# Zero matmuls in TensorE's waits, and ScalarE's tables held to the set with both Ln and Exp, in a two-block transformer kernel

## The chip, the core and the metric

The kernel runs on one core of one Trainium2 chip. TensorE multiplies into PSUM, VectorE and ScalarE read PSUM and work in SBUF, GpSimd helps VectorE, and DMA queues bring the weights from HBM. The metric is the device time of one execution in microseconds (us). Before the change it is 2707.82 us, the median of 3 runs (2706.88 to 2712.28).

## The reference

All is fp32, for 256 tokens of width 1024, in two blocks.

```python
# first block, layers l = 0, 1
x = x + (swa_sb_mixer(h, ...) if l == 0 else hgrn2_mixer(h, ...))   # h = rms_norm(x, norm_mix[l])
x = x + memory_cross_attention(rms_norm(x, norm_cross[l]), rms_norm(mem, norm_mem[l]), ...)
x = x + conv_ffn(rms_norm(x, norm_ffn[l]), ...)
# second block, i = 0, 1
h = pool_mixer(x, ...) if i == 0 else nsa_mixer(x, ...)
x = layer_norm(ALPHA * x + h, ln_g[i, 0], ln_b[i, 0])
f = swiglu(x, ...) if i == 0 else moe_ffn(x, ...)        # 8 experts, each token goes to 2
x = layer_norm(ALPHA * x + f, ln_g[i, 1], ln_b[i, 1])
```

The first mixer is a sliding-window softmax (8 heads) beside stick-breaking attention (8 heads: softplus, a reversed cumulative sum, exp). HGRN2 is gated linear attention with a decay. NSA has three branches: keys compressed by a small network, selected blocks, and a window; here the last two are causal attention over all 256 keys, 4 groups of 4 heads.

## The kernel before, in words

**Layout.** Activations stand with channels on the 128 partitions: `x` is 8 blocks of 256 tokens. All dense weights come as one stream of slots of 128x2048 fp32 (1 MB). SyncE loads a slot into one of 6 `raw` buffers, ScalarE rounds it to fp32r (`whi`, `split_hi`, line 458, 4 buffers), VectorE or GpSimd subtracts (`wlo`, lines 1294 and 426), and TensorE makes three matmuls of each product: high by high, high by low, low by high (`split_mm`, lines 722 to 724). The activations are split the same way into `hh` and `hl` (`to_hi`, `to_lo`, lines 1359 and 1362).

**Stages, in the order of the program.** ab_in (9 slots), sliding window, stick-breaking, ab_out (4); cross-attention with kv (8 slots), q (4), o (4); feed-forward (33); HGRN hg_in (16), its chunk products, hg_out (4); cross-attention and feed-forward again; then pool (1), LayerNorm 0, feed-forward, LayerNorm 1, nsa_in (10), the compressed branch, the NSA softmax, nsa_out (4), LayerNorm 2, router, 8 experts of 42 slots, LayerNorm 3. A projection slot is 48 matmuls of 128x256: 2 output blocks of 8 input blocks of 3.

**What sets the order.** Each engine runs its own list, written out by hand, and waits for semaphores. There is no scheduler. TensorE runs its list in order, so whatever stands in front of a wait is done before the wait is looked at, and whatever stands behind waits too.

**A norm.** VectorE squares (line 1338), TensorE sums over channels with a matrix of ones in fp32 (line 776; each such matmul is two instructions in the trace), ScalarE makes rstd as exp(-0.5 ln(sum)) (lines 471 and 472), VectorE scales (line 1372) and splits in four quarters (semaphore `h_ready`), and the first 24 matmuls of the next slot wait for these quarters one after the other. A LayerNorm (`layer_norm_pe`) has two such sums, of x and of the centred squares, and scales and shifts (lines 1401, 1406) before the split.

**Softmax stages** (`softmax_pe`, `softmax_act`, `softmax_dve`). In each step TensorE makes the scores of a unit of 4 heads (line 817), the transposes of the probabilities two units back (line 803) and the value product three units back (lines 846, 854, 857). VectorE masks and takes the maximum (lines 1432 to 1440), ScalarE makes four Exp (line 487) and then the copy of the transposes (line 496).

**ScalarE's tables.** The build puts an ACT_TABLE_LOAD ahead of an activation whose function is not in the set that is loaded. Where Ln and Exp follow each other it loads for each of them.

Of the kernel before, what the change touches and what calls it, by code (L numbers as in the profile page):

```python
# [14 lines left out]
P = 128  # L15
# [3 lines left out]
BLK = T  # L19
SLOT = 16 * P  # L20
QUARTERS = 4
# [81 lines left out]
def build(nc, stream, x_in, mem_in, pos_in, params, consts, stage_consts, w1_in, out):  # L103
    ctx = ExitStack()
    with ctx:
# [338 lines left out]
        def _(act):  # L444
# [22 lines left out]

            def norm_act(n, count, eps):
# [7 lines left out]

            def softmax_act(kind, u0):
                us = units(kind)
                for step in range(len(us) + 2):
# [11 lines left out]
                    if step >= 2:  # L491
# [4 lines left out]
                        nc.scalar.activation(r3(PT[u % 2], 4)[:, :, 0:nk], r3(banks(2), 4)[:, :, 0:nk], ACT.Copy).then_inc(pt_copied, 1)  # L496

            def ffn_act(layer, conv):
                for i in range(4):
# [5 lines left out]
                    for s in range(ph.n):  # L505
# [6 lines left out]
                        split_hi(ph.g + s + DEPTH)  # L512

# [32 lines left out]
            nc.scalar.activation(W(33, 2), W(33, 2), ACT.Sin).then_inc(sines_ready, 1)  # L546

# [36 lines left out]
            def log_decays():  # L584
                act.wait_ge(hg_sig, 1)
# [37 lines left out]
            nc.scalar.activation(W(24, 8), W(24, 8), ACT.Silu).then_inc(hg_gate, 1)  # L623
            for c in range(QUARTERS):
                act.wait_ge(hg_o, c + 1)
                nc.scalar.activation(hf[:, c * 512:(c + 1) * 512], ps[:, c, :], ACT.Square).then_inc(hg_osq, 1)
# [28 lines left out]
            ins.then_inc(cmp_silu, 1)  # L655
            act.wait_ge(cmp_shifted, 1)
# [45 lines left out]
            with act.Else():  # L702
# [9 lines left out]
                expert_pairs(act, expert)  # L712
            norm_act(11, D, 1e-5)
# [3 lines left out]
        def _(pe):  # L717
# [8 lines left out]
            def proj_slot(ph, s, e=0, h=None, odd=0):  # L726
# [15 lines left out]
            def proj_pe(name, h, then=None):  # L742

                ph = PHASES[name]
                for s in range(ph.n):
                    proj_slot(ph, s, h=h)
# [40 lines left out]
            def ffn_pe(layer, h):  # L787
                at_least(pe, acc_drained, QUARTERS * layer)
                for i in range(4):
                    ph = PHASES[f"ffn{layer}_{i}"]  # L790
                    if ph.kind == "gu":
                        for s in range(ph.n):
                            proj_slot(ph, s, h=h if i == 0 else None)
# [11 lines left out]
            def softmax_pe(kind, u0, o0, q_at, k_at, v_at, cmp=None):  # L805
                us = units(kind)
                branches = 2 if kind == "nsa" else 1
                for step in range(len(us) + 3):
                    if step < len(us):
                        u = u0 + step  # L810
                        g, qt, br = us[step]
                        nk = P * key_tiles(kind, qt)
                        at_least(pe, scores_masked, u)
# [16 lines left out]
                    if step >= 3:  # L830
# [3 lines left out]
                        kts = key_tiles(kind, qt)  # L834
# [1340 lines left out]
```

## Time and profile before

| | us |
|---|---|
| median of 3 runs | 2707.82 (2706.88 to 2712.28) |
| profiled execution | 2710.58 |
| its span, first to last instruction | 2708.8 |
| TensorE (PE) busy | 2463.7 (91%), 17928 instructions |
| VectorE (DVE) busy | 1854.6 (68%) |
| ScalarE (ACT) busy | 1322.4 (49%) |
| GpSimd (POOL) busy | 309.4 (11%) |
| mean granted clock of TensorE | 0.948 of full |

The granted clock has two levels: 1.00 is 2.4 GHz, 0.50 is 1.2 GHz. Busy TensorE counts pipelined matmuls that overlap, so it does not say that the array runs at its peak. PEld rows are weight loads. An idle time in brackets is that of the engine ahead of the row, and the name behind the arrow is what ended it. Idle time of an engine that nobody waits for costs nothing.

### The profile page before, as it was taken

The numbers are of one execution on the slowest core, as the hardware profiler recorded it, in microseconds if no ns is written. First come the engines' busy times: TensorE is split into PE (matmuls) and PEld (weight loads), VectorE is DVE, ScalarE is ACT, GpSimd is POOL, SyncE is SP. The second block draws the span as 40 slices with busy tenths as digits, with TensorE's granted clock in tenths as the row PEclk, the third lists the DMA queues.
The fourth block names the chain that finished last, engine by engine and source line by source line (L and its number), as shares of the span: only waits on it lengthen the run. The fifth ranks groups of instructions, "written<-read, shape, count | busy, mean of one in ns | idle before, by whom it ended". The sixth has DMA issues, their size and how long they took to land.

```text
span 2708.8 us, 43109 instructions
## 1 busy us (share of the span) xinstructions
PE 2463.7 (91%) x17928; PEld 2323.5 (86%) x17928; DVE 1854.6 (68%) x2338; ACT 1322.4 (49%) x1432; POOL 309.4 (11%) x70
## 2 busy tenths in 40 slices
PE   6779789988887899699988888999999999999997
PEld 6579789988887899699987568999999999999996
DVE  5655466668565675723355657888888888888887
ACT  4443333344433333233321435766767677676764
POOL 0000054500000364163400000000000000000000
PEclk9789899999998899899988799999999999999998
DMA  5124135442341355355531015988989998899995
GB/s 210 63 80 154 63 141 187 179 143 107 108 150 63 125 184 179 110 182 181 187 109 47 1 63 200 362 339 327 353 333 343 344 343 344 340 345 342 342 341 207
DMA packets 77087, 556.69 MB, mean 206 GB/s; under 512 B 8544, under 2 KB 8672, under 8 KB 9952
## 3 DMA queue, kind: packets, MB, share of 16 engines
q1 hardware_dynamic: 75888, 547.45, 54.8%
q10 hardware_dynamic: 1008, 6.49, 0.6%
q8 instruction: 145, 2.38, 0.3%
q14 instruction: 46, 0.38, 0.1%
HBM read 552.86 MB, written 1.05 MB: 204 GB/s over the span
## 4 chain that ended last, share of the span: by engine, by line
PE 61%; DVE 4%; ACT 2%; issue 1%; DMA 0%; ACTq 0%; DVEq 0%
PE ps L1169 11%; PE ps L1171 11%; PE ps L1170 11%; PE ps L722 6%; PE ps L723 6%; PE ps L724 6%; PE ps L803 2%; PE ps L776 1%; PE ps L1209 1%; PE ps L1163 1%; PE ps L857 1%; PE ps L817 1%; PE ps L854 1%; ACT whi L458 0%; PE ps L1081 0%
## 5 line engine op out<-in xcount | busy, mean ns | idle before, releaser
L458 ACT ACTIVATE whi<-raw 128x2048 fp32r<-128x2048 f32 x519 | 994.1, 1916 | 658.0 <-PE ps L724 505.4
L1294 DVE TENSOR_TENSOR wlo<-raw,whi 128x2048 fp32r<-128x2048 f32 x453 | 1035.0, 2290 | 226.1 <-ACT whi L458 225.4
L722 PE MATMUL ps<-hh,whi 128*128 128x256 f32 x2336 | 678.8, 291 | 98.6 <-DVE hl L1362 90.2
L723 PE MATMUL ps<-hl,whi 128*128 128x256 f32 x2336 | 672.1, 288 | 0.0
L724 PE MATMUL ps<-hh,wlo 128*128 128x256 f32 x2336 | 671.5, 287 | 0.0
L722 PEld LDWEIGHTS ps<-hh,whi 128*128 128x128 f32 x2336 | 460.0, 197 | 105.0 <-issue 103.2
L1169 PE MATMUL ps<-whi,hh 128*128 128x256 f32 x1792 | 523.4, 292 | 3.6 <-DVE work L1939 3.6
L1171 PE MATMUL ps<-wlo,hh 128*128 128x256 f32 x1792 | 507.7, 283 | 0.0
L1170 PE MATMUL ps<-whi,hl 128*128 128x256 f32 x1792 | 507.6, 283 | 0.0
L723 PEld LDWEIGHTS ps<-hl,whi 128*128 128x128 f32 x2336 | 460.4, 197 | 0.3
L724 PEld LDWEIGHTS ps<-hh,wlo 128*128 128x128 f32 x2336 | 459.8, 197 | 0.0
L426 POOL TENSOR_TENSOR wlo<-raw,whi 128x2048 fp32r<-128x2048 f32 x66 | 309.2, 4684 | 1018.3 <-ACT whi L458 1018.3
L1169 PEld LDWEIGHTS ps<-whi,hh 128*128 128x128 f32 x1792 | 343.4, 192 | 4.4 <-DVE work L1939 3.8
L1170 PEld LDWEIGHTS ps<-whi,hl 128*128 128x128 f32 x1792 | 344.7, 192 | 0.6
L1171 PEld LDWEIGHTS ps<-wlo,hh 128*128 128x128 f32 x1792 | 344.1, 192 | 0.0
L1169 PE MATMUL ps<-whi,ahi 128*128 128x512 f32 x448 | 180.8, 404 | 0.0
L1171 PE MATMUL ps<-wlo,ahi 128*128 128x512 f32 x448 | 174.7, 390 | 0.0
L1170 PE MATMUL ps<-whi,alo 128*128 128x512 f32 x448 | 174.6, 390 | 0.0
L723 PE MATMUL ps<-alo,whi 128*128 128x256 f32 x528 | 149.4, 283 | 0.0
L724 PE MATMUL ps<-ahi,wlo 128*128 128x256 f32 x528 | 149.4, 283 | 0.0
L722 PE MATMUL ps<-ahi,whi 128*128 128x256 f32 x528 | 149.4, 283 | 0.0
L686 ACT ACTIVATE work<-ps 128x128 f32<-128x128 f32 x224 | 62.3, 278 | 165.3 <-PE ps L1171 165.2
(319 smaller groups left out, 2681.1 us busy)
## 6 DMA issues: line engine op xcount, KB each, us to landing
raw<-stream SPq DMA_DIRECT2D x519, 1024.0 KB, 4.8
work<-w_in ACTq DMA_DIRECT2D x1, 2240.0 KB, 8.4
stage<-stage_consts ACTq DMA_DIRECT2D x4, 512.0 KB, 4.8
work<-mem_in ACTq DMA_DIRECT2D x2, 1024.0 KB, 4.8
x<-x_in SPq DMA_DIRECT2D x1, 1024.0 KB, 4.9
out<-x SPq DMA_DIRECT2D x4, 256.0 KB, 2.3
const<-consts SPq DMA_DIRECT2D x1, 548.5 KB, 5.8
par<-params SPq DMA_DIRECT2D x1, 405.5 KB, 6.4
```

Of the source, the lines that this page charges most:

```text
L426: nc.gpsimd.tensor_tensor(wlo[g % RAWS][:, :], raw[g % RAWS][:, :], whi[hi_at(g, odd)][:, :].bitcast(F32), ALU.subtract).then_inc(lo_ready ...
L458: nc.scalar.activation(whi[hi_at(g, odd)][:, :], raw[g % RAWS][:, :], ACT.Copy).then_inc(hi_ready, 1)
L686: nc.scalar.activation(Wc(FEW_GATE + P * bank, P), ps[:, bank, 0:P], ACT.Silu).then_inc(gate_act, 1)
L722: mm(out_ap, hi_w, hi_x, start=start, stop=False, **kw)
L723: mm(out_ap, hi_w, lo_x, start=False, stop=False, **kw)
L724: return mm(out_ap, lo_w, hi_x, start=False, stop=stop, **kw)
L776: last = mm(ps[:, bank, 0:BLK], C("ones"), src[:, b * BLK:(b + 1) * BLK], start=(b == 0), stop=(b == NB - 1))
L803: return nc.tensor.transpose(dst, src, C("ident"))
L1169: mm(out_ap, hi_x, hi_w, start=start, stop=False, **kw)
L1170: mm(out_ap, lo_x, hi_w, start=False, stop=False, **kw)
L1171: return mm(out_ap, hi_x, lo_w, start=False, stop=stop, **kw)
L1294: V.tensor_tensor(wlo[g % RAWS][:, :], raw[g % RAWS][:, :], whi[hi_at(g, odd)][:, :].bitcast(F32), ALU.subtract).then_inc(lo_ready[g % RAW ...
```

## The change

**TensorE.** `keep_warm(bank, n)` issues n matmuls of a tile of zeros (128x128) by zeros (256 columns, fp32r) into a bank that nobody reads at that time. It stands ahead of waits: 12 to 32 at the start of projections (with `norm`, 6 ahead of a wait for rstd, the rest behind it), 4 ahead of each group of scores, transposes and values in the sliding window and in NSA, 8 in cross-attention, 12 and 8 in stick-breaking, 24 and 16 in pool, 14 to 24 between the sums of a LayerNorm, and a few more. They are 948 in all. A few waits are new or come earlier (`xa_rstd`, `hg_orstd`, `rstd_ready`, `dup_copied`), each of something that a later wait implies.

**ScalarE.** `load_log_exp` loads the set that has both Ln and Exp, `load_exp` the set of Exp that the softmaxes had before. After them the build finds the functions loaded and adds nothing. 43 loads run where 61 ran. The first layer is not restored after the sliding window, so norms 1 and 2, stick-breaking and the first cross-attention load as before. VectorE's, GpSimd's and SyncE's lists are the same.

```diff
+            def load_log_exp():
+
+                act.preload_act_table_set("natural_log_exp_and_others")
...
+            def load_exp():
+
+                act.preload_act_table_set("exp_and_others")
+
             def softmax_act(kind, u0):
+                load_exp()
...
+                if kind != "swa":
+                    load_log_exp()
...
                         split_hi(ph.g + s + DEPTH)
+                    if i == 2:
+                        load_log_exp()
...
             def log_decays():
+                load_log_exp()
...
             nc.scalar.activation(W(24, 8), W(24, 8), ACT.Silu).then_inc(hg_gate, 1)
+            load_log_exp()
...
+            def keep_warm(bank, n):
+
+                for _ in range(n):
+                    mm(ps[:, bank, 0:BLK], zero[:, :], zero[:, :].unsqueeze(1).to_broadcast([P, 2, P]), start=True, stop=True)
+
-            def proj_slot(ph, s, e=0, h=None, odd=0):
+            def proj_slot(ph, s, e=0, h=None, odd=0, idle=0, norm=None):
...
+                if norm is not None:
+                    keep_warm(bank, 6)
+                    pe.wait_ge(rstd_ready, norm + 1)
+                keep_warm(bank, idle)
...
-            def layer_norm_pe(i, wait):
+            def layer_norm_pe(i, wait, idle):
                 sums_pe(x, MEAN_BANK[i], wait).then_inc(mean_ready, 1)
+                keep_warm(7, idle)
                 norm_pe(8 + i)
...
+                def warm(step, n):
+                    if kind != "xa":
+                        keep_warm(7, n)
+                    elif step < 3:
+                        keep_warm(4, 2 * n)
...
+                        if step:
+                            warm(step, 4)
                         at_least(pe, scores_masked, u)
...
+                        warm(step, 4)
                         pe.wait_ge(probs_ready, u + 1)
...
+                        warm(step, 4)
                         pe.wait_ge(pt_copied, u + 1)
...
+                pe.wait_ge(xa_rstd, 3 * layer + 3)
+                keep_warm(4, 20)
                 pe.wait_ge(heads_ready, 2 + layer)
...
-            proj_pe("hg_in", 7, {s: lambda s=s: after_hg_slot(s) for s in range(7, hg.n)})
+            proj_pe("hg_in", 7, idle=22, norm=4, then={s: lambda s=s: after_hg_slot(s) for s in range(7, hg.n)})
             pe.wait_ge(banks_drained, hg.e + hg.n)
+            keep_warm(0, 10)
...
-            proj_pe("hg_out", 8, {1: lambda: norm_pe(5)})
+            pe.wait_ge(hg_orstd, QUARTERS)
+            keep_warm(7, 16)
+            proj_pe("hg_out", 8, then={1: lambda: norm_pe(5)})
...
-            ffn_pe(1, 12)
+            ffn_pe(1, 12, norm=7, idle=22)
+            keep_warm(7, 24)
...
             for g in range(4):
+                keep_warm(7, 16 if g else 24)
                 pe.wait_ge(h_ready, QUARTERS * 12 + g + 1)
...
+            keep_warm(7, 10)
             pe.wait_ge(cmp_kv_copied, 1)
             mm(ps[:, 3, 0:60], C("rot"), small[:, 288:348], start=True, stop=True).then_inc(cmp_rot, 1)
+            keep_warm(7, 8)
             pe.wait_ge(cmp_roped, 1)
...
-            layer_norm_pe(3, lambda c: pe.wait_ge(acc_drained, QUARTERS * 3 + c + 1))
+            keep_warm(7, 8)
+            layer_norm_pe(3, lambda c: pe.wait_ge(acc_drained, QUARTERS * 3 + c + 1), 20)
```

TensorE's list from the end of the first feed-forward over norm 4 to hg_in, before (line 767 closes the accumulation, 776 is the norm's sums, 722 to 724 the projection):

```order
L767 MATMUL ps<-zero 128x512 x4
L776 MATMUL ps<-hf,const 128x256 x8
L722 MATMUL ps<-hh,whi_63 128x256
L723 MATMUL ps<-hl,whi_63 128x256
L724 MATMUL ps<-hh,wlo_57 128x256
```

and with the change, where the same lines are 794, 803 and 740 to 742, and 747 is `keep_warm`:

```order
L794 MATMUL ps<-zero 128x512 x4
L747 MATMUL ps<-zero 128x256 x10
L803 MATMUL ps<-hf,const 128x256 x8
L747 MATMUL ps<-zero 128x256 x28
L740 MATMUL ps<-hh,whi_63 128x256
L741 MATMUL ps<-hl,whi_63 128x256
L742 MATMUL ps<-hh,wlo_57 128x256
```

Ten stand ahead of the sums, 6 + 22 between them and the first matmul that waits for h.

ScalarE's list at the HGRN output norm, before (626 squares, 630 is Ln, 633 Exp):

```order
L623 ACTIVATE work<-work 128x2048
L626 ACTIVATE hf<-ps 128x512 x4
L630 ACT_TABLE_LOAD
L630 ACTIVATE work<-ps,const 128x512 x4
L633 ACT_TABLE_LOAD
L633 ACTIVATE work<-work 128x512 x4
```

and with the change:

```order
L638 ACTIVATE work<-work 128x2048
L470 ACT_TABLE_LOAD
L642 ACTIVATE hf<-ps 128x512 x4
L646 ACTIVATE work<-ps,const 128x512 x4
L649 ACTIVATE work<-work 128x512 x4
```

One load is left, and it has moved ahead of the squares.

TensorE's list in the NSA softmax, before (817 scores, 803 transposes, 854 and 857 values):

```order
L857 MATMUL ps<-probs_t,work 64x128 x4
L817 MATMUL ps<-work 128x128 x4
L803 MATMUL ps<-const,hf 128x128 x8
L854 MATMUL ps<-work,rstd 64x128
L857 MATMUL ps<-probs_t,work 64x128 x2
```

and with the change (855 scores, 832 transposes, 894 and 897 values):

```order
L897 MATMUL ps<-probs_t,work 64x128 x4
L747 MATMUL ps<-zero 128x256 x4
L855 MATMUL ps<-work 128x128 x4
L747 MATMUL ps<-zero 128x256 x4
L832 MATMUL ps<-const,hf 128x128 x8
L747 MATMUL ps<-zero 128x256 x4
L894 MATMUL ps<-work,rstd 64x128
L897 MATMUL ps<-probs_t,work 64x128 x2
```

Each of the three groups of a step has four zero matmuls in front of it.

## Rows read from the trace of the kernel before

**Rows 1.** The page's head: span, busy time by engine, granted clock in 40 slices
```profile
span 2708.8 us, 43109 instructions
...
PE 2463.7 (91%) x17928; PEld 2323.5 (86%) x17928; DVE 1854.6 (68%) x2338; ACT 1322.4 (49%) x1432; POOL 309.4 (11%) x70
...
PEclk9789899999998899899988799999999999999998
```

**Rows 2.** The page: chain that ended last, by engine
```profile
PE 61%; DVE 4%; ACT 2%; issue 1%; DMA 0%; ACTq 0%; DVEq 0%
```

**Rows 3.** Windows: stretch, its length, busy time by engine, granted clock, DMA
```profile
252.60:256.00 3.40, 3.40 (x18) 3.40 (x18) 1.77 (x1) 0.00 (x0) 0.00 (x0) 0.50 0.00 0
256.10:262.10 6.00, 6.00 (x54) 6.00 (x53) 3.14 (x3) 1.92 (x1) 0.00 (x0) 1.00 0.31 126
...
1490.00:1584.00 94.00, 77.38 (x480) 51.12 (x480) 59.76 (x162) 41.13 (x144) 0.00 (x0) 0.77 0.00 1
...
1649.00:2677.00 1028.00, 1027.41 (x7279) 967.49 (x7280) 883.33 (x812) 722.90 (x790) 0.00 (x0) 1.00 0.91 342
```

**Rows 4.** Windows of all 38 stretches at clock 0.50: first, one, sum
```profile
23.92:34.16 10.24, 4.50 (x19) 4.24 (x20) 7.00 (x16) 1.78 (x3) 0.00 (x0) 0.50 0.00 0
...
703.17:706.58 3.41, 3.41 (x18) 3.41 (x18) 0.75 (x1) 0.60 (x1) 0.00 (x0) 0.50 0.00 0
...
sum 276.44, PE 199.51 PEld 164.87 DVE 171.40 ACT 61.05 POOL 4.47; mean PE 5.25 PEld 4.34 DVE 4.51 ACT 1.61 POOL 0.12
```

**Rows 5.** Timeline of norm 4: start, length, engine, line, operation, [idle before <-releaser]
```profile
553.46 4.39 PE L776 MATMUL ps<-hf,const 128*128 128x256 f32 x16 [1.98 <-DVE hf L1338]
...
557.89 0.47 ACT L471 ACTIVATE rstd<-ps,const 128x256 f32<-128x256 f32 x1 [4.03 <-PE ps L776]
558.38 1.28 ACT L472 ACT_TABLE_LOAD   x1
559.68 0.42 ACT L472 ACTIVATE rstd<-rstd 128x256 f32<-128x256 f32 x1
560.21 1.67 DVE L1372 SCALAR_TENSOR_TENSOR hf<-x,par,rstd 128x256 f32<-128x256 f32 x4 [3.80 <-ACT rstd L472]
...
563.26 0.68 DVE L1362 TENSOR_TENSOR hl<-hf,hh 128x512 fp32r<-128x512 f32 x1
...
564.09 0.55 PE L722 MATMUL ps<-hh,whi 128*128 128x256 f32 x1 [6.23 <-DVE hl L1362]
```

**Rows 6.** ScalarE's groups by line: count | busy, mean ns | idle before
```profile
L472 ACT ACT_TABLE_LOAD x12 | 15.4, 1283 | 0.2
```

**Rows 7.** Timeline of the second cross-attention: head norm, scores, first transposes
```profile
846.90 1.67 DVE L1559 SCALAR_TENSOR_TENSOR work<-work,par 128x256 f32<-128x256 f32 x4 [0.96 <-ACT work L533]
848.63 6.04 PE L817 MATMUL ps<-work 128*128 128x256 f32 x16 [4.43 <-DVE work L1559]
...
863.79 1.97 PE L803 MATMUL ps<-const,work 128*128 128x128 f32 x8 [4.03 <-DVE work L1455]
```

**Rows 8.** Timeline of the pool stage: first matmul, sums behind the four groups
```profile
1126.76 0.55 PE L722 MATMUL ps<-hh,whi 128*128 128x256 f32 x1 [15.85 <-DVE hl L1362]
...
1133.95 3.62 PE L776 MATMUL ps<-x,const 128*128 128x256 f32 x16
```

**Rows 9.** Timeline of the HGRN output norm: load between Ln and Exp
```profile
714.08 1.28 ACT L633 ACT_TABLE_LOAD   x1
```

**Rows 10.** Timeline of the compressed branch: its scores
```profile
1464.76 7.01 PE L1102 MATMUL ps<-small,work 64*128 64x15 f32 x64 [0.82 <-DVE small L1593]
```

**Rows 11.** Timeline of the NSA softmax: two waits for ScalarE's copy
```profile
1525.15 0.63 PE L803 MATMUL ps<-const,work 128*128 128x128 f32 x4 [2.74 <-ACT probs_t L496]
...
1547.57 0.63 PE L803 MATMUL ps<-const,hf 128*128 128x128 f32 x4 [2.74 <-ACT probs_t L496]
```

**Rows 12.** Timeline of stick-breaking: ScalarE's Exp of the second unit
```profile
144.02 1.06 ACT L568 ACTIVATE probs_t<-work 128x1024 f32<-128x1024 f32 x1 [2.12 <-DVE work L1658]
```

**Rows 13.** Timeline of the last LayerNorm: sums of squares
```profile
2692.88 5.41 PE L776 MATMUL ps<-hf,const 128*128 128x256 f32 x16 [2.18 <-DVE hf L1338]
```

More of the change, by code:

```diff
@@ L740, in proj_slot, with proj_pe @@
                 last.then_inc(slot_used, 1)
-            def proj_pe(name, h, then=None):
+            def proj_pe(name, h, then=None, idle=0, norm=None):
                 ph = PHASES[name]
                 for s in range(ph.n):
-                    proj_slot(ph, s, h=h)
+                    proj_slot(ph, s, h=h, idle=0 if s else idle, norm=None if s else norm)
                     if then is not None and s in then:
@@ L780, in norm_pe, with ffn_pe @@
                 sums_pe(hf, 7, lambda c: pe.wait_ge(squares_ready, QUARTERS * n + c + 1)).then_inc(sums_ready, 1)
-            def layer_norm_pe(i, wait):
+            def layer_norm_pe(i, wait, idle):
                 sums_pe(x, MEAN_BANK[i], wait).then_inc(mean_ready, 1)
+                keep_warm(7, idle)
                 norm_pe(8 + i)
-            def ffn_pe(layer, h):
+            def ffn_pe(layer, h, norm, idle):
                 at_least(pe, acc_drained, QUARTERS * layer)
@@ L792, in ffn_pe @@
                         for s in range(ph.n):
-                            proj_slot(ph, s, h=h if i == 0 else None)
+                            first = i == 0 and s == 0
+                            proj_slot(ph, s, h=h if i == 0 else None, idle=idle if first else 0, norm=norm if first else None)
                         a0 = ph.a
@@ L862, in xa_pe @@
             def xa_pe(layer, h):
-                proj_pe(f"kv{layer}", h, {1: lambda: norm_pe(layer * 4 + 2)})
+                proj_pe(f"kv{layer}", h, idle=22, then={1: lambda: norm_pe(layer * 4 + 2)})
                 def turn_values():
@@ L885, in key_sums @@
                     head_sums_of(1, W(32, 8), range(4), 4)
-                proj_pe(f"q{layer}", h + 1, {0: turn_values, 1: key_sums,
+                proj_pe(f"q{layer}", h + 1, idle=22, then={0: turn_values, 1: key_sums,
                                              2: lambda: head_sums_of(3, hf, (0, 1), 6),
                                              3: lambda: head_sums_of(5, hf, (2, 3), 6)})
+                pe.wait_ge(xa_rstd, 3 * layer + 3)
+                keep_warm(4, 20)
                 pe.wait_ge(heads_ready, 2 + layer)
@@ L894, in xa_pe @@
                            lambda g, h, kt, eb: Wc(6144 + kt * 1024 + (2 * h + eb) * P, P))
-                proj_pe(f"o{layer}", h + 2)
+                proj_pe(f"o{layer}", h + 2, idle=16)
             pe.wait_ge(params_loaded, 32)
@@ L919, in swa_key_copies @@
                 last.then_inc(dup_ready, 1)
-            proj_pe("ab_in", 1, {3: swa_sums, 5: swa_half_turns, 7: swa_key_copies})
+            proj_pe("ab_in", 1, idle=14, norm=0, then={3: swa_sums, 5: swa_half_turns, 7: swa_key_copies})
             pe.wait_ge(banks_drained, PHASES["ab_in"].e + PHASES["ab_in"].n)
@@ L968, in _ @@
             norm_pe(3)
-            ffn_pe(0, 6)
+            ffn_pe(0, 6, norm=3, idle=22)
+            keep_warm(7, 10)
             norm_pe(4)
@@ L1040, in _ @@
                 last.then_inc(pool_ps if g < 3 else slot_used, 1)
-            layer_norm_pe(0, lambda c: pe.wait_ge(pool_added, c + 1) if c < 3 else pe.wait_ge(banks_drained, ph.e + 1))
-            ffn_pe(2, 14)
-            layer_norm_pe(1, lambda c: pe.wait_ge(acc_drained, QUARTERS * 2 + c + 1))
+            layer_norm_pe(0, lambda c: pe.wait_ge(pool_added, c + 1) if c < 3 else pe.wait_ge(banks_drained, ph.e + 1), 24)
+            ffn_pe(2, 14, norm=8, idle=32)
+            layer_norm_pe(1, lambda c: pe.wait_ge(acc_drained, QUARTERS * 2 + c + 1), 14)
             e_nsa = PHASES["nsa_in"].e
@@ L1083, in hidden_layers @@
                 last.then_inc(cmp_hidden, 1)
-            proj_pe("nsa_in", 15, {6: group_copies, 7: gates_and_query_turns, 8: hidden_layers})
+            proj_pe("nsa_in", 15, idle=32, norm=9, then={6: group_copies, 7: gates_and_query_turns, 8: hidden_layers})
             pe.wait_ge(banks_drained, e_nsa + PHASES["nsa_in"].n)
```

12 lines of the change are left out of this document (11 added, 1 removed).

## The prediction

> **What bounds the kernel now.** I read the page's head first. The span is 2708.8 us, and the row of TensorE's granted clock stands below 9 in ten of its 40 slices, nine of them among the first 23, and the last [rows 1]. The chain that ended last is TensorE's for 61% of the span, with 4% of VectorE and 2% of ScalarE [rows 2]: what TensorE does, or waits for, is the time. The windows view then splits the span. From 1649 to 2677 us, in the eight experts, TensorE is busy for 1027.41 of 1028.00 us at clock 1.00 [rows 3]. The change puts nothing there, so 1028 us stand as they are, and all that can move lies in the first 1649 us and the last 32.
>
> Asked for the 38 stretches at clock 0.50 alone, the same view sums 276.44 us, with TensorE busy for 199.51 [rows 4]. What is half a clock worth? At 0.50, 18 projection matmuls touch 3.40 us, at 1.00, 54 touch 6.00 us [rows 3]; each is shown for longer than its place in the stream, so two to four of each count belong to an edge, which leaves one every 0.21 us and one every 0.12 us. An fp32 matmul of 256 columns goes at 0.43 against 0.22. So the 199.5 us hold 90 to 95 us, if the clock never fell and if each matmul were on the path. Neither holds, and the working below asks at each place who is late when TensorE is not.
>
> **Table loads.** The change has 43 where 61 ran, at 1.28 us each. A load ahead of a semaphore's wait runs while ScalarE idles and is free: the one before Ln is such. The one between Ln and Exp is not. In norm 4 Ln ends at 558.36, the load runs from 558.38 to 559.66, Exp starts at 559.68, VectorE at 560.21 [rows 5]. It costs 1.30 us on a chain on which TensorE has nothing else. Twelve norms load there [rows 6]. Four of them stand between slots of a projection and are hidden, eight (0, 3, 4, 7 and the four LayerNorms) end in a wait of TensorE: 8 x 1.30 = 10.4 us. The load between the four Ln and the four Exp of the HGRN output norm [rows 9] and the one in the last head norm of the second cross-attention add 2.6. In the first layer the set is not restored after the sliding window, so its cross-attention and the stick-breaking keep theirs. Loads that are new (after each softmax, after the third feed-forward phase) meet an idle ScalarE. Sum 13.0 us.
>
> The Trainium skill (ScalarE: Activation LUTs, "What ACT_TABLE_LOAD costs") puts a drain of 1380 ns beside the load, 2.66 us for a switch. By that the ten would be worth 26.6 us and the kernel would take 2662. The trace does not agree: it shows 0.02 us on either side of the load [rows 5], and I give that time no chance.
>
> **Starts of projections.** One dummy (256 columns, zeros) has no row of its own. The nearest are the projection's matmuls of the same width, and I take their 0.12 us at 1.00 and 0.21 at 0.50 [rows 3]; the ends are 0.11 (54 in 6.00 us) and 0.21 throughout, the last of which is a rival below. In norm 4 TensorE's sums end at about 557.85 and hg_in starts at 564.09 after 6.23 us [rows 5]. Without the load the wait is 4.9 us; 6 + 22 dummies take 3.4 of it, with holes of 0.4 and 1.1 us. I expect clock 1.00 at the start. What does it give? The first 24 matmuls need the four quarters of h, which VectorE delivers at 0, 1.7, 2.6 and 3.3 us (the first ends at 563.94 [rows 5], the others by the rows behind it). Cold, 24 x 0.21 = 5.1 us plus a hole of 0.3 is TensorE's own pace; warm, they end 0.72 us after the last quarter, at 4.0. So 1.4 us come from there and 0.2 from the cold matmuls behind: 1.6, not the 2.5 that 26 x 0.094 suggests. In the same way, from the other cold stretches of that view and VectorE's pace: first and second feed-forward 1.5 and 1.7, HGRN output 1.2, kv 0.5 and 1.1, q 1.6 and 0.4, second o 1.5, third feed-forward and nsa_in 1.0 each (a LayerNorm delivers quarters slowly), ab_in 0.5 (its dummies follow Exp, after some 5 us of nothing). Sum 13.6 us.
>
> **Attention.** Cross-attention scores start cold: 6.04 us for 16 fp32 instructions in the second layer [rows 7] against 3.5 warm. But 20 dummies wait for the head norm (2.4 us) where VectorE needs 1.7 until the scores may start [rows 7]: 0.7 too long. Second layer 2.5 - 0.7 = +1.8; in the first, where the load stays and leaves a longer hole ahead, the dummies may themselves run cold (4.3 us): 0. The wait of 4.03 us before the first transposes [rows 7] gets 8 dummies, 1.0 us, and 3 us of nothing; the transposes and value matmuls behind it hold about 3 us of half clock per layer, of which I take 40%: 2.5. Stick-breaking: TensorE's twelve instructions of a unit take 5.1 cold and 2.6 warm (at 0.43 and 0.22), but ScalarE waited for them 2.12 us in one unit [rows 12] and less in the others, and 8 dummies (1.0) stand ahead of each value product: +2.5. HGRN's products: 18 instructions in a cold stretch of 3.41 us [rows 4] at half: +1.5. Compressed scores: 64 small instructions take 7.01 us at 0.50 [rows 10] and VectorE waits for just them: 3.5 less 0.2 of dummies: +3.3. Sum 11.6.
>
> The NSA softmax runs 16 units in some 92 us with the clock at 0.77 in the mean [rows 3]. Its loop, over two units, is scores, VectorE's mask and maximum, ScalarE's four Exp and its copy of the transposes two units back, then TensorE's transposes, values and next scores; the 2.74 us that TensorE waits for that copy [rows 11] show that it is a chain and not throughput. Four units take 22.42 us from 1525.15 to 1547.57 [rows 11]; all warm I get some 20.1 (the cold value products and scores on the loop), 2.3 less. Against that 4 + 4 dummies stand on the loop, between transposes and values and between values and scores: 0.96 per two units, 1.9 per four. Only the four ahead of the transposes are covered by the wait. Net 0, ends -4 and +6; likewise 0 for the sliding window, which VectorE bounds.
>
> **Where dummies cost.** In the pool stage TensorE waits 15.85 us [rows 8], which 48 dummies cannot bridge, so it starts cold. Then 16 stand ahead of each of three groups. Now the four groups end 7.2 us after the start, back to back, and the sums follow at 1133.95 [rows 8]: TensorE is late there, not VectorE. 3 x 16 x 0.12 = 5.8, more while cold: -6.3, ends -5 and -10. At the end, 8 dummies precede sums that now follow without a hole (-1.0) and 20 (2.4 us) fill a wait of 2.18 [rows 13] (-0.2). LayerNorm sums, which VectorE paces, give back +1.3.
>
> **The sum.** 13.0 + 13.6 + 1.8 + 2.5 + 2.5 + 1.5 + 3.3 + 0 - 6.3 - 1.2 + 1.3 = 32.0 us. The span becomes 2676.8. The profiled execution took 2710.58 us, 1.8 over its span and 2.8 over the median of 2707.82; taken off that median, 2675.8: I predict 2676.
>
> **Rivals.**
> Warmer than forecast. The pauses of the cross-attention stay at 1.00 (+4), NSA's loop proves to hold more cold work than I took (+6), the first layer's head norm fits (+2), pool's dummies overlap VectorE's additions (+4). Against it: the holes of 3 us that stay. About 48 us, 2660. Chance 0.17.
>
> Half of the clock is given back. The loops of NSA and the sliding window pay for dummies (-8), pool -10, q and kv stay cold after the last hole (-4). The loads' 13 us remain and about 4 of the rest: 2691. For it: TensorE is on the chain for 61% [rows 2], so each dummy that is not covered costs fully. Chance 0.13.
>
> Slower: the clock does not answer to zeros. Then all cold stretches stay, and 948 dummies run at 0.21 in most of their places. The place that decides is the NSA loop: 8 per two units at 0.21 is 1.7, 14 us in all; norms' 28 take 6.0 us where 4.9 are open (1 us each, 7); pool 10; head norms 5; stick-breaking 6; the rest 3. 45 - 13 = 32 us slower, 2740. It decides from the first projection: no matmul rate above one per 0.21 us there. Against: projection matmuls of the same form run at 0.50 at first and at 1.00 a few us on [rows 3], and nothing in the trace ties that to what they multiply. Chance 0.05. On this the Trainium skill (TensorE: Matmul & The Clock Gate, Part 1) says that the clock is throttled by default and released by activity, and it makes operands of zeros an exception only for a current limiter that three busy cores of a die trip; no run here shows either.
>
> No change that can be measured (0.2%, 5.4 us, is about what a measurement of this kernel tells): dummies eat exactly the gain. 2706, chance 0.04.
>
> The forecast itself has 0.61. Only the last two rivals are not faster: faster 0.91, same 0.04, slower 0.05. The range for 8 in 10 takes the first rival's middle and most of the second: 2655 to 2699.
>
> **What would show it.** Right: mean granted clock of 0.97 or more against 0.948; ScalarE busy about 23 us less; Exp 0.02 us behind Ln in norm 4 and a wait of 4.9 us there; hg_in's first matmuls 0.12 apart; pool's four groups spread over 13 us instead of 7; NSA's 16 units in 88 to 96 us; the expert stage within 1 us of 1028. Wrong: clock 0.50 behind dummies, new waits of VectorE for TensorE in the softmax loops, or less than 10 us from the loads.

## The result and the profile after

The changed kernel takes 2684.98 us (median of 4 runs, 2679.80 to 2686.25) against 2710.05 of the kernel before in the same comparison (4 runs). The ratio is 0.9906, with a 95% interval of 0.9892 to 0.9920: 25 us faster. The forecast was 2676 in a range of 2655 to 2699. Sign and range held. Of the 9 us between them 2.2 are the kernel before, which stood at 2710.05 here and at 2707.82 where the forecast began. The rest is the gain: 32 us were forecast, 25 came by the medians and 26 by the profile.

The head of the page of the changed kernel, to be held against [rows 1]:

```profile
span 2682.7 us, 44984 instructions
...
PE 2539.2 (95%) x18876; PEld 2407.3 (90%) x18876; DVE 1857.9 (69%) x2338; ACT 1299.7 (48%) x1414; POOL 309.7 (12%) x70
...
PEclk9899999999999999899998999999999999999999
...
PE ps L1225 11%; PE ps L1227 11%; PE ps L1226 11%; PE ps L740 8%; PE ps L741 8%; PE ps L742 8%; PE ps L832 2%; PE ps L747 1%; PE ps L803 1%; PE ps L1219 1%; PE ps L1265 1%; PE ps L897 1%; PE ps L1040 1%; PE ps L855 1%; ACT whi L458 1%
```

ScalarE is busy 22.7 us less, about the 18 loads of 1.28 that are gone. The mean granted clock is 0.980 (0.948 before). Asked for the stretches at clock 0.50, the windows view lists 21 where [rows 4] has 38, and their last row is:

```profile
sum 102.40, PE 89.86 PEld 80.92 DVE 64.55 ACT 17.66 POOL 0.00; mean PE 4.28 PEld 3.85 DVE 3.07 ACT 0.84 POOL 0.00
```

TensorE's busy time at the lower clock fell by 110 us (199.51 before, 89.86 now, dummies among it), and the kernel gained 26 in its profile. A dummy is one of `keep_warm`'s matmuls of zeros. They have a row of their own in the groups by line; L747 is `keep_warm`:

```profile
L747 PE MATMUL ps<-zero 128*128 128x256 f32 x948 | 149.3, 305 | 13.9 <-ACT rstd L476 6.7
```

Norm 4 shows a place where it went as forecast, to be held against [rows 5]. These are its rows in the timeline of the changed kernel (start, duration, engine, line):

```profile
548.80 3.64 PE L803 MATMUL ps<-hf,const 128*128 128x256 f32 x13
...
552.10 1.06 PE L747 MATMUL ps<-zero 128*128 128x256 f32 x6
552.48 0.48 ACT L475 ACTIVATE rstd<-ps,const 128x256 f32<-128x256 f32 x1 [5.33 <-PE ps L803]
552.99 0.42 ACT L476 ACTIVATE rstd<-rstd 128x256 f32<-128x256 f32 x1
553.46 2.89 PE L747 MATMUL ps<-zero 128*128 128x256 f32 x22 [0.31 <-ACT rstd L476]
553.52 1.67 DVE L1429 SCALAR_TENSOR_TENSOR hf<-x,par,rstd 128x256 f32<-128x256 f32 x4 [2.52 <-ACT rstd L476]
...
557.31 0.38 PE L740 MATMUL ps<-hh,whi 128*128 128x256 f32 x1 [0.97 <-DVE hl L1419]
557.54 0.28 PE L741 MATMUL ps<-hl,whi 128*128 128x256 f32 x1
557.65 0.28 PE L742 MATMUL ps<-hh,wlo 128*128 128x256 f32 x1
```

Exp follows Ln at once. The holes are 0.31 and 0.97 us, and hg_in's matmuls follow each other in 0.12 us. The first 24 take 4.20 us, from the start of the first to the start of the 25th, where they took 5.64. That holds in nine of the ten profiles of kernels that have both parts of the change there. In the tenth, of the kernel without pool's 16 dummies, which runs the same instructions up to this point, the clock fell behind the first quarter and the 24 took 5.48 (columns: us, busy time of each engine, granted clock):

```profile
558.30:562.00 3.70, 3.70 (x19) 3.70 (x20) 2.91 (x11) 0.22 (x1) 0.00 (x0) 0.54 0.00 0
```

So even a wait that is filled keeps the clock in most executions and not in all.

A mark such as "first matmul of ffn2" has a time in each profile. The changed kernel's lead at such marks, taken stage by stage, stands beside the forecast's terms, sorted into the same stages:

| stage, up to | forecast | measured |
|---|---|---|
| ab_in | 1.8 | 1.5 |
| sliding window | 0 | -2.8 |
| stick-breaking | 2.5 | 4.4 |
| ab_out, kv, q | 2.1 | 2.2 |
| first cross-attention | 1.3 | 0.2 |
| o, norm 3, start of ffn0 | 2.8 | -0.1 |
| norm 4, start of hg_in | 2.9 | 2.9 |
| HGRN's products, start of hg_out | 4.0 | 4.2 |
| second kv, q | 1.5 | 3.0 |
| second cross-attention | 4.3 | 3.3 |
| o, norm 7, start of ffn1 | 4.5 | 2.4 |
| pool, LayerNorm 0, start of ffn2 | -3.4 | -5.1 |
| LayerNorm 1, start of nsa_in | 2.6 | 2.7 |
| compressed branch | 3.3 | 3.5 |
| NSA softmax | 0 | -3.8 |
| nsa_out, LayerNorm 2, router | 1.7 | 3.8 |
| experts, last spreads, LayerNorm 3 | 0.1 | 3.7 |
| sum | 32.0 | 26.0 |

Six places are off by over 2 us. The two softmax loops and the two feed-forward starts (2.9 and 2.1) fell short; the router and the end gave more.

### The profile page after: what moved, and what is told of

The parts are those of the page before. It is cut to its first block, busy times and chain, and to the rows that moved or that the text cites. A ratio compares the mean times of both kernels' runs of the same rounds, so it can differ in the third digit from the quotient of the medians.

```text
span 2682.7 us, 44984 instructions
## 1 busy us (share of the span) xinstructions
PE 2539.2 (95%) x18876; PEld 2407.3 (90%) x18876; DVE 1857.9 (69%) x2338; ACT 1299.7 (48%) x1414; POOL 309.7 (12%) x70
## 4 chain that ended last, share of the span: by engine, by line
PE 68%; DVE 5%; issue 2%; ACT 2%; DMA 0%; DVEq 0%; ACTq 0%
PE ps L1225 11%; PE ps L1227 11%; PE ps L1226 11%; PE ps L740 8%; PE ps L741 8%; PE ps L742 8%; PE ps L832 2%; PE ps L747 1%; PE ps L803 1%; PE ps L1219 1%; PE ps L1265 1%; PE ps L897 1%; PE ps L1040 1%; PE ps L855 1%; ACT whi L458 1%
## 5 line engine op out<-in xcount | busy, mean ns | idle before, releaser
L741 PE MATMUL ps<-hl,whi 128*128 128x256 f32 x2336 | 665.4, 285 | 0.0
L740 PEld LDWEIGHTS ps<-hh,whi 128*128 128x128 f32 x2336 | 452.6, 194 | 44.5 <-DVE hl L1419 38.8
L741 PEld LDWEIGHTS ps<-hl,whi 128*128 128x128 f32 x2336 | 453.2, 194 | 0.3
L742 PEld LDWEIGHTS ps<-hh,wlo 128*128 128x128 f32 x2336 | 452.9, 194 | 0.0
L747 PE MATMUL ps<-zero 128*128 128x256 f32 x948 | 149.3, 305 | 13.9 <-ACT rstd L476 6.7
L747 PEld LDWEIGHTS ps<-zero 128*128 128x128 f32 x948 | 128.5, 201 | 29.5 <-issue 11.3
```

The lines of the kernel that those rows point to most:

```text
L740: mm(out_ap, hi_w, hi_x, start=start, stop=False, **kw)
L741: mm(out_ap, hi_w, lo_x, start=False, stop=False, **kw)
L742: return mm(out_ap, lo_w, hi_x, start=False, stop=stop, **kw)
L747: mm(ps[:, bank, 0:BLK], zero[:, :], zero[:, :].unsqueeze(1).to_broadcast([P, 2, P]), start=True, stop=True)
```

## The experiments

Their lines are numbered a few off the changed kernel's. Each was timed against the kernel before, at 2710.8 to 2711.1 us.

**Tables alone.** In the changed kernel `keep_warm` makes no matmul:

```diff
-                for _ in range(n):
+                for _ in range(0):
```

> Of the change only the pinned tables and the few waits that came with the dummies; no matmul of zeros. My theory: each load between Ln and Exp was 1.30 us of a chain on which TensorE waited, ten such places, 13 us: about 2697 against 2710, ratio 0.9952, and Exp 0.02 us behind Ln in the norms that are covered. Rival A: some of the loads were hidden behind something that is late next (VectorE's work, weights), the gain is under 8 us: above 2702. Rival B: a switch costs more than its 1.28 us row, 2.66 us in all: about 2683. The clock's cold stretches stay at some 38 with 276 us.

Measured: 2693.95 us, ratio 0.9943 (0.9930 to 0.9956), runs from 2686.7 to 2697.5. It gained 17 us, between my figure and rival B's. The trace shows 1.28 per place and not 2.66: from the last sum to the first matmul it takes 5.33 instead of 6.61 us in norm 4, and 7.62 instead of 8.90 in the first two LayerNorms; the last LayerNorm's end gives the same. Four other places took 1.0 to 1.9 us less, with changes of the clock in it. In norms 3 and 7 it takes 8.61 as before: rival A, at two of ten places. So eight loads give about 10.3. In the profile more came from the clock, without a dummy: stick-breaking took 38.0 us instead of 42.7, HGRN's products 5.4 instead of 7.1 to the norm's sums, the last spreads 2.7 less. The mean clock was 0.955 instead of 0.948. But the profiled run was the fastest of the six, 7 us under their median, so these three gains need not be there in every run. How the 6.5 us that the median has beyond the loads come about is not shown.

**Dummies alone.**

```diff
-                act.preload_act_table_set("natural_log_exp_and_others")
+                pass
...
-                act.preload_act_table_set("exp_and_others")
+                pass
```

> The changed kernel without the pinned tables: 948 matmuls of zeros, and the build's own loads (61). My theory: the trace of the changed kernel gave 25 us, of which ten loads are 13; the dummies alone are worth 12: about 2698 against 2710. By the terms of the prediction it would be 19 (2691). Rival: the two parts work together, since each dummy that fits into a wait fits into a longer one as well (the wait for rstd is 1.3 us longer with the load in it, so that the hole behind six dummies is longer and the clock falls again): under 8 us, above 2702.

Measured: 2707.97, ratio 0.9988 (0.9978 to 0.9997), 12 runs from 2696.91 to 2710.28. The rival's number, and its reason is not what cost most. In norm 4 the hole behind the six dummies is 1.59 us instead of 0.31 and the clock does fall, but it fell there with a hole of 0.31 too, in the tenth profile above. At the first scores of the NSA softmax this kernel leads the kernel before by 9.4 us, not far from my theory's 12, and in that softmax it loses 9.4. The window of the 16 units, first in this kernel, then in the changed one (columns: us, busy time of each engine, granted clock):

```profile
1481.86:1581.56 99.70, 96.11 (x651) 72.45 (x648) 58.50 (x158) 41.15 (x144) 0.00 (x0) 0.88 0.00 1
```

```profile
1468.89:1562.96 94.07, 91.19 (x653) 68.91 (x650) 58.61 (x158) 42.45 (x145) 0.00 (x0) 0.93 0.00 1
```

The same instructions, TensorE busy for 96% or 97% of either, and 5.6 us apart: in the first more of them ran at 0.50. With the 90.3 us that this loop takes in the kernel before, the dummies would have been worth about 12 us (2.8 and 9.4), not 3.

**No dummies in the two loops.** In `warm`:

```diff
-                    if kind != "xa":
-                        keep_warm(7, n)
-                    elif step < 3:
+                    if kind == "xa" and step < 3:
```

> The changed kernel without the dummies in the loops of the sliding window and of the NSA softmax (those of cross-attention stay). My theory: on these loops a dummy is on the path of the next unit, and what the clock gives back is less. In the changed kernel's trace the NSA softmax lost 3.7 us on the kernel before and the sliding window 2.8; without them both are as before: 6.5 us faster than the changed kernel, about 2678.5, and the NSA units 1502 to 1526 take 22.4 per four instead of 23.7. Rival A: the dummies were free and the loss comes from elsewhere (a bank, ScalarE): no difference, 2685. Rival B: they hold the clock for what follows (stick-breaking, nsa_out, LayerNorm 2, router): it loses that and ends at 2683 to 2688.

Measured: 2681.50, ratio 0.9896 (0.9881 to 0.9912), between my figure and rival B's. The profile leads the changed kernel by 6.9 us up to the experts, 0.4 more than the theory's 6.5; the sliding window (to stick-breaking's first scores) took 25.1 us instead of 28.3 and NSA 90.35 instead of 94.06. At the end 3.4 us of this went again, where the edit touches nothing: the wait ahead of the last spreads was 2.0 longer, for a reason that is open, and 9 of their 16 instructions ran at 0.50, which cost 1.4. What dummies do on the loop can be read in the changed kernel. [Rows 11] show the wait that they were to fill; these are the rows behind it:

```profile
1507.35 1.23 PE L855 MATMUL ps<-work 64*128 64x128 f32 x8
1508.51 1.22 PE L747 MATMUL ps<-zero 128*128 128x256 f32 x4
1508.63 0.69 DVE L1489 SCALAR_TENSOR_TENSOR work<-ps,stage 128x512 f32<-128x512 f32 x1 [2.85 <-PE ps L855]
...
1509.53 1.31 PE L832 MATMUL ps<-const,hf 128*128 128x128 f32 x8
...
1510.59 0.72 PE L747 MATMUL ps<-zero 128*128 128x256 f32 x4
...
1511.24 0.66 PE L897 MATMUL ps<-probs_t,work 128*64 128x128 f32 x8
...
1511.83 1.00 ACT L505 ACTIVATE probs_t<-ps 128x1024 f32<-128x1024 f32 x1
```

VectorE waited 2.85 us for the scores, and four dummies stood in front of them. The four in front of the value product delay the next scores. A group of four takes 0.65 us to the next instruction at 1.00 (from 1510.59) and 1.02 at 0.50 (from 1508.51), where I had put 0.48, and the clock fell in spite of them.

**No dummies between pool's groups.**

```diff
-                keep_warm(7, 16 if g else 24)
+                if g == 0:
+                    keep_warm(7, 24)
```

> The changed kernel without the 3 x 16 dummies between pool's four groups (24 ahead of the first stay). My theory: TensorE was late there, so each was on the path: 3 x 16 x 0.12 to 0.21 is 5.8 to 6.7 us, about 2679 against 2685, the four groups back to back in some 7 us again. Rival A: they paid in part by warming what follows (groups 1 to 3 and the sums of LayerNorm 0): half, about 2682. Rival B: VectorE's additions behind the groups are late in any case: no gain, 2685.

Measured: 2680.41, ratio 0.9895 (0.9879 to 0.9910). From pool's first matmul to the first of ffn2 it takes 28.37 us where the changed kernel has 34.94: 6.6 us by the profile, of which 2.4 is lost again at the last spreads. In the changed kernel the first group and the dummies behind it, to be held against [rows 8]:

```profile
1105.41 0.58 PE L740 MATMUL ps<-hh,whi 128*128 128x256 f32 x1 [10.01 <-DVE hl L1419]
...
1108.14 3.21 PE L747 MATMUL ps<-zero 128*128 128x256 f32 x16
...
1111.19 0.28 PE L740 MATMUL ps<-hh,whi 128*128 128x256 f32 x1
...
1112.62 2.08 PE L747 MATMUL ps<-zero 128*128 128x256 f32 x16
1112.82 0.88 DVE L1870 SCALAR_TENSOR_TENSOR x<-ps,par,x 128x256 f32<-128x256 f32 x2 [2.34 <-PE ps L742]
```

The first 16 take 3.21, nearly all of it at 0.50, the next 2.08 at 1.00, and VectorE has become the one that waits.

**The same two kernels once more.** Both unchanged, one profile each.

> The kernel before, unchanged, profiled once more. Theory (phase): where the clock falls and rises does not stand still against the program, so the same instructions are at 1.00 in one execution and at 0.50 in the next. The tables-only kernel, without a single zero matmul, ran stick-breaking in 38.0 us (first scores to the next projection) where the kernel before took 40.3, as fast as the changed kernel with its 12 and 8 dummies (38.3). Then this profile has at least one stage that differs from the first profile by over 1 us (stick-breaking, norm starts, or the last spreads), and single executions lie anywhere within 2703 to 2714 us. Rival: the clock follows the program exactly; every stage repeats within 0.3 us, and stick-breaking takes 40.3 us again.

Measured: 2712.51. The phase theory holds in small: the first 24 matmuls of the first o took 4.43 us where they took 2.95, those of the first q 4.19 instead of 5.26. Stick-breaking took 43.2 (42.7 by the same marks in the first profile; the 40.3 of my expectation was read from another mark). Over the whole kernel the two profiles are never more than 2.0 us apart.

> The changed kernel, unchanged, profiled once more. Theory (phase): the starts of the fully covered waits repeat (hg_in at 1.00), but the places with a hole of some us do not: in the dummies-only kernel the NSA softmax lost 9.7 us on the kernel before, in the changed kernel 3.7, at the same instructions. Here it loses something between 3 and 10, and the last spreads take 1.9 us (at 1.00) or some 5 (at 0.50). Time 2679 to 2687. Rival: the NSA softmax takes 94.1 us again within 0.3, and the difference to the dummies-only kernel has to do with ScalarE's tables.

Measured: 2685.53. My theory missed for NSA: 94.04 us after 94.06. The rival was right on the repeat. Stick-breaking took 40.0 instead of 38.3.

**The kernel shifted in front of NSA.** 10 or 20 dummies more, in the middle of nsa_in, where TensorE never waits:

```diff
-            proj_pe("nsa_in", 15, idle=32, norm=9, then={6: group_copies, 7: gates_and_query_turns, 8: hidden_layers})
+            proj_pe("nsa_in", 15, idle=32, norm=9, then={3: lambda: keep_warm(7, 10), 6: group_copies, 7: gates_and_query_turns, 8: hidden_layers})
```

> The changed kernel with 10 dummies more inside nsa_in, behind slot 3: 1.1 us later from there on, nothing else. The NSA softmax (16 units, with 4 dummies ahead of scores, transposes and values) took 94.06, 94.04 and 94.07 us in three profiles and 99.71 in the dummies-only kernel, which reached it 12 us later. Theory (phase): what it takes depends on when it starts against the clock's falls; moved by 1.1 us it takes another time than 94.1 (by over 1 us), 88 to 100. Rival: 94.1 again, and the 99.7 has to do with the tables after all.

Measured: 2685.91, NSA 94.15: rival.

> The same with 20 dummies, 2.1 us later. Theory (phase): at least one of the two shifts gives another time for the NSA softmax than 94.1 by over 1 us. Rival: both give 94.1 within 0.3, and the whole kernel is later by just 2.1 us.

Measured: 2687.19, NSA 91.23 at a clock of 0.96, over 1 us from 94.1, as the theory said of at least one of the two:

```profile
1471.81:1563.03 91.22, 88.55 (x651) 66.64 (x648) 58.47 (x158) 42.44 (x145) 0.00 (x0) 0.96 0.00 1
```

With ScalarE's tables as in the changed kernel and 20 dummies more ahead of it, this loop took 2.8 us less. So the same instructions can take 91.2 or 94.1. That the start decides is not shown by it: the loop started at 1462.7, 1468.9, 1470.1 and 1470.7 us in four profiles that gave 94.0 to 94.2, and at 1471.8 in this one. Why the dummies-only kernel has 99.7 stays open; that it meets a worse case of the same kind is my guess.

**On-path dummies removed.** The last two changes together, no 8 ahead of the last sums, 14 for 20 in cross-attention, and 24 in the wait ahead of the last spreads:

```diff
-                keep_warm(4, 20)
+                keep_warm(4, 14)
...
+                keep_warm(0, 24)
                 pe.wait_ge(y_kept, EXPERTS)
                 few_spread(EXPERTS - 1, 0, 5)
...
-            keep_warm(7, 8)
             layer_norm_pe(3, lambda c: pe.wait_ge(acc_drained, QUARTERS * 3 + c + 1), 20)
```

> The changed kernel without the dummies that stand on the path: none in the loops of the sliding window and NSA, none between pool's groups, no 8 ahead of the last sums, 14 instead of 20 ahead of the first cross-attention scores; and 24 new ones in the wait of 3 us ahead of the last two spreads. Theory: the gains of the two runs without loop dummies (6.9 us up to the experts) and without pool's 16s (5.9) add, 1 us from the last sums, 0.7 from each head norm, and the last spreads stay at 1.00 (up to 3.8 us in executions in which they fell): about 2671 against 2685 for the changed kernel, ratio 0.9855. Rival: the two gains overlap or what follows pool and the loops gets colder: 2676 to 2680.

Measured: 2670.82 (2670.53 to 2671.51), ratio 0.9858 (0.9843 to 0.9873). The gains add. The last spreads held 1.00, and the runs lie within 1 us.

**Dummies where TensorE waits.** On top of that:

```diff
-                        warm(step, 4)
+                        keep_warm(*((7, 4) if kind != "xa" else (4, 30 if step == 2 else 0)))
                         pe.wait_ge(probs_ready, u + 1)
```

> As the kernel with the on-path dummies removed, plus dummies only where TensorE waits: 4 ahead of each group of transposes in the sliding window and NSA (the wait of 2.7 us for ScalarE's copy), and 30 instead of 8 ahead of the first transposes of cross-attention (a wait of 4 us). Theory: what stands in a wait costs nothing and holds part of the clock: NSA's loop 1 to 3 us faster than without any, transposes and values of the two cross-attentions 1 us each: 2667 to 2669. Rival: four dummies are too few to keep the loop's matmuls at 1.00, and they are late in some units: same as or up to 2 us slower than the kernel without them, 2671 to 2673.

Measured: 2667.84 (2663.52 to 2669.97), ratio 0.9844 (0.9831 to 0.9858). NSA takes 87.3 us and each cross-attention, from its first scores to the next projection, 2.4 and 2.6 less:

```profile
1458.56:1545.86 87.30, 78.93 (x528) 56.37 (x527) 58.52 (x158) 42.44 (x145) 0.00 (x0) 0.84 0.00 1
```

The clock in NSA is 0.84 here and 0.93 in the changed kernel, and it is 6.8 us faster. These three places give 8.1 us, but the profile is only 2.8 faster than that of the kernel before this step: stick-breaking took 40.2 us instead of 38.3, and other places that the edit does not touch moved by up to 1.3 either way.

**GpSimd out of the norm's way.** On top of that, in GpSimd's list:

```diff
+                    if ph.name in ("ffn0_0", "ffn1_0"):
+                        pool.wait_ge(h_ready, QUARTERS * (6 if ph.name == "ffn0_0" else 12))
                     for s in range(ph.n):
                         split_lo(ph.g + s + AHEAD)
```

> The kernel with dummies only in waits (2667.8), and one thing more: ahead of the first and the second feed-forward GpSimd starts its first subtraction of a slot only when the norm's four quarters are written. Theory: GpSimd's subtraction and VectorE's SCALAR_TENSOR_TENSOR exclude each other. In norm 3 the first of VectorE's eight takes 2.48 us before the change, 3.76 with the tables pinned, 3.85 in the changed kernel, and ends at the same distance from the last sum in all of them, since it waits for the end of GpSimd's 5.9 us; the others take 0.47. That is where the loads of norms 3 and 7 went (the time from the last sum to the feed-forward's first matmul is 8.61 us in every kernel so far). Without the subtraction beside it the first takes 0.47, and that time falls to 5.2: 3.4 us twice, 6.8, less what GpSimd now disturbs a little later: 2661 to 2663. Rival A: the subtraction only moves and blocks VectorE's split or drains instead: gain under 2 us, above 2666. Rival B: slot 3 comes too late for TensorE, and it is slower: above 2669.

Measured: 2653.89 (2652.11 to 2656.98), ratio 0.9794 (0.9780 to 0.9808): 14 us faster than the one before by the medians, twice what I expected. Its profiled run was the slowest of the five, and gains 10.9. The first SCALAR_TENSOR_TENSOR of norm 3 (ns, then its start) in four kernels: before, tables alone, changed, and all eight in this one.

```profile
L1372 DVE SCALAR_TENSOR_TENSOR hf<-x,par,rstd x1: 2481/2481/2481, 351.1 to 351.1; 128x256 f32<-128x256 f32 x1
```

```profile
L1429 DVE SCALAR_TENSOR_TENSOR hf<-x,par,rstd x1: 3759/3759/3759, 343.6 to 343.6; 128x256 f32<-128x256 f32 x1
```

```profile
L1429 DVE SCALAR_TENSOR_TENSOR hf<-x,par,rstd x1: 3853/3853/3853, 344.4 to 344.4; 128x256 f32<-128x256 f32 x1
```

```profile
L1430 DVE SCALAR_TENSOR_TENSOR hf<-x,par,rstd x8: 480/483/485, 337.6 to 341.7; 128x256 f32<-128x256 f32 x8
```

And GpSimd's subtraction beside it, before (with one of VectorE's ahead of it), changed, and in this kernel, where it starts behind the split:

```profile
346.66 2.29 DVE L1294 TENSOR_TENSOR wlo<-raw,whi 128x2048 fp32r<-128x2048 f32 x1
347.38 5.93 POOL L426 TENSOR_TENSOR wlo<-raw,whi 128x2048 fp32r<-128x2048 f32 x1 [346.93 <-ACT whi L458]
```

```profile
341.92 6.02 POOL L426 TENSOR_TENSOR wlo<-raw,whi 128x2048 fp32r<-128x2048 f32 x1 [341.47 <-ACT whi L458]
```

```profile
344.73 4.62 POOL L426 TENSOR_TENSOR wlo<-raw,whi 128x2048 fp32r<-128x2048 f32 x1 [344.28 <-DVE hl L1420]
```

GpSimd ends at 353.31 and VectorE's instruction at 353.58 before; 347.94 and 348.21 in the changed kernel. Each time it is 0.27 us behind. Without the load VectorE starts 1.28 earlier and stands for 1.28 longer. With the subtraction away, last sum to first matmul falls from 8.61 to 5.25 us in both norms (6.7), and since the dummies now reach as far as hg_in's do, both feed-forwards start at 1.00 (first 24 in 4.20 instead of 4.88 and 5.74, which is 2.2 us). The Trainium skill (SBUF — State Buffer, "SBUF: two separate sides") says that VectorE, in an instruction with two SBUF inputs, and a GpSimd instruction that reads SBUF take a shared port pair as an exclusive lock for a whole instruction, and the loser blocks. That VectorE's instruction ends 0.27 us behind GpSimd's in both profiles agrees with it. What the runs show by themselves is that VectorE's instruction is long where the two meet and short where they do not; the port as the reason is the page's.

By the profiles the lead over the previous kernel was 14.5 us at the end of NSA. Of these the edit accounts for 8.9 (6.7 and 2.2). The other 5.6 came in steps of 0.2 to 1.7 us, and a few back, at places that it does not touch (ab_in, HGRN's output, the second kv, the start of ffn2, the compressed branch), so how much of the 14 us belongs to the edit is not shown beyond the 8.9. In the first expert 3.0 went again: it starts before its weights are there. ScalarE's roundings in 1655 to 1715 us, which waited 8.0 for them (2.4 in the previous kernel):

```profile
L460 ACT ACTIVATE whi<-raw 128x2048 fp32r<-128x2048 f32 x19 | 36.4, 1916 | 12.8 <-DMA raw<-stream 8.0 <-PE ps L1228 4.9
```

**Without stick-breaking's dummies.**

```diff
-                    keep_warm(7, 12)
                     pe.wait_ge(sp_ready, u + 1)
...
-                    keep_warm(7, 8)
                     pe.wait_ge(a_ready, u + 1)
```

> As the kernel in which GpSimd waits in front of the feed-forwards, without the 12 and 8 dummies of stick-breaking. Stick-breaking took 42.7 and 43.2 us in the two profiles of the kernel before, 38.0 in the tables-only kernel (no dummies either), and 38.3 or 40.0 to 40.3 in the seven profiles with dummies. Theory: without them it takes 38 or 43 by how the clock's falls lie; the dummies are worth 2 to 3 us on average, and single executions spread more: 2 to 3 us slower than with them, or spread over 5 us. Rival: they are worth nothing once the tables are pinned: the same time within 1 us, and 38.0.

Measured: 2655.28 (2653.78 to 2656.83), ratio 0.9799 (0.9785 to 0.9813): 1.4 us more than with them, which the runs' spread (2652.11 to 2656.98) does not let one call a difference. The stage took 37.9 us, 2.1 less than with the dummies, at a clock of 0.86 instead of 0.96. With these dummies it took 38.3 to 40.3 in ten profiles, without them 42.7, 43.2, 38.0, 37.9, the last two with the tables pinned. The rival holds for the stage; for the whole kernel 2 us either way are not excluded.

## Why the prediction was right, and where its sizes were off

**The clock answers to zeros.** Right: the granted clock rose from 0.948 to 0.980, and to 0.972 with the dummies alone. The slower rival is out: dummies run at 0.12 us, and projections behind them too. The 0.12 and 0.21 us taken for a dummy from the projection's matmuls [rows 3] held in norm 4 and in pool.

**Table loads, 13.0.** The step "twelve norms load there, eight end in a wait of TensorE: 8 x 1.30" failed at norms 3 and 7. I saw TensorE wait and ScalarE between, but never looked at VectorE's own time, where one instruction of eight took 2.48 us and not 0.47. GpSimd was late there. 10.3 us remain. That there is no further drain beside a load held: norm 4 and three LayerNorms gave 1.28 us each, not 2.66.

**Starts of projections, 13.6.** In this profile they gave 9.6. Where VectorE set the pace from rows that I had worked out (hg_in, HGRN output, second o), the terms held within 0.2 us (1.44 of 1.6, 1.24 of 1.2, 1.47 of 1.5). But for the second o this is partly luck: its 24 took 2.95 us in the tables-only kernel too, without a dummy, where the kernel before took 4.44. The terms failed in ffn0 (1.5 forecast, 0 measured) and partly ffn1 (0.9 of 1.7), since with GpSimd in the way the wait was 8.6 us where 28 dummies fill 4. In ffn2 the first 24 took 5.04 after 4.66, so nothing came of its 1.0, and nsa_in gave 0.15 of 1.0.

**The loops, 0 and 0.** The largest error, 6.6 us, and more than the 6.0 between the two sums; the others cancel. I netted "2.3 us gained, 1.9 spent per four units" in NSA. The 1.9 assumed dummies at 0.12 us, and the gain assumed that they hold the clock, and neither held in all turns: three stretches at 0.50 remained, with dummies in each. My low end of -4 for it was nearly reached (-3.8). For the sliding window "which VectorE bounds" was no reason to put nothing: dummies ahead of scores delay VectorE too.

**Stick-breaking, 2.5.** The stage gave 4.4, but the tables-only kernel gave 4.7 there without a dummy, and in the last experiment the stage was no slower without them. That a gain came where one was forecast is luck. What took the stage from 43 to 38 us in those two kernels is open: its own loads were the same.

**Pool, -6.3.** Right: -6.7 at the sums, and 6.6 came back when they were taken out.

**Cross-attention, 4.3.** 2.2 (the table's 0.2 and 3.3, less the load of 1.3 that stood with it). The first layer lost 1.9 us before its scores, with 12 of the 20 dummies at 0.50: the prediction named that case and put it at 0.

**The end, -1.2.** The 8 dummies cost 0.9 to 1.5 us in seven profiles. What I had not seen are the two last spreads: 16 instructions of fp32 matmuls behind a wait of 3.3 us, which run at either clock. In both profiles of the changed kernel they ran at 1.00 and took 3.72 us instead of 6.41; in four variants (dummies alone, no loop dummies, no pool dummies, shift by 20) they did not, and took 5.35 to 6.60. In the router, where I had put only the load, matmuls behind short waits moved to 1.00 as well, 2.3 us, of which 1.7 came in the tables-only kernel too.

## What to carry to other kernels

Fill only waits whose length is known to be longer than the dummies, and put none ahead of an instruction that a loop waits for: a lower mean clock with 4 dummies in the wait beat a higher one with 12, eight of them on the loop's path, by 6.8 us. Before a shortened chain is counted as a gain, look at the durations of single instructions on it and not only at who waits: one of eight equal ones that takes 2.5 us instead of 0.5 says that another engine is late. An effect that rides on the clock should be read from several profiles, since the same instructions took 1 to 5 us more or less from one profile to the next.

## What was not expected of the hardware

VectorE's scaling instruction, when it comes later than GpSimd's subtraction, lasts until 0.27 us behind that one's end, in both kernels, and the profile shows this as its own duration and not as idle time. GpSimd's subtraction takes 5.93 to 6.02 us here, where its median over the kernel before is 4.63:

```profile
L426 POOL TENSOR_TENSOR wlo<-raw,whi x66: 4612/4632/5927, 347.4 to 1323.3; 128x2048 fp32r<-128x2048 f32 x66
```

It had itself started 1.57 us before the end of a subtraction of VectorE's (346.66 and 2.29 above), so it looks as if it had waited as well; no run takes that one away by itself.

Stick-breaking without dummies took 42.7 and 43.2 us at a mean clock of 0.76 and 0.80, or 38.0 and 37.9 at 0.87 and 0.86. NSA's loop took 90.0 to 90.4 us in five profiles without dummies, 91.2 to 99.7 in six with 4 ahead of each of its three groups, and 86.5 to 87.3 in three with 4 ahead of the transposes alone. The loop with the most dummies on its path spreads most. I read this as TensorE on the path making the time hang on where the clock's falls lie; no run separates the two.
